# Moving four modulation units from the first MLP to the Hyena block of a diffusion backbone

## What is computed

```python
def adaln(cond, w, b):
    return jnp.split(jax.nn.silu(cond) @ w + b, 6, axis=-1)     # w: 2048 x 12288, per layer
...
sh1, sc1, g1, sh2, sc2, g2 = adaln(c[:, None, :], mod_w[l], mod_b[l])
...
# layer 1 (odd):
y = hyena_mixer(modulate(x, norm_mix_g[l], sh1, sc1), od_w_in[o], ...)
x = x + g1 * (y @ od_w_out[o])
x = x + g2 * ffn(modulate(x, norm_ffn_g[l], sh2, sc2), ffn_w1[l], ffn_w2[l])
...
def hyena_mixer(h, w_in, conv_w, conv_b, filt, skip):
    p = depthwise_conv(h @ w_in, conv_w) + conv_b
    x0, x1, v = jnp.split(p, 3, axis=-1)
    return x0 * bidir_long_conv(x1 * v, filt, skip)
def ffn(h, w1, w2):
    return jnp.square(jax.nn.relu(h @ w1)) @ w2
```

## Time and profile before

| | |
|---|---|
| median of 3 runs | 2666.0 us |
| profiled execution: device time | 2669.68 us |
| its span, first to last instruction | 2667.9 us |
| PE busy | 2517.2 us (94%) |
| DVE busy | 1812.4 us (68%) |
| ACT busy | 955.7 us (36%) |
| moved from memory | 611.40 MB, 229 GB/s |
| mean granted TensorE clock | 0.969 |
| first MLP, from its first to its last matmul | 694.11 to 1441.75 us |
| Hyena block, from its first matmul to the output projection's first | 1456.51 to 1797.61 us |

### The profile page before, as it was taken

One profiled execution on the slowest core, in us unless ns is written; L12 is line 12 of the kernel. 1 busy time (PEld: TensorE's weight loads), 2 busy tenths in 40 slices (PEclk: granted clock), 3 DMA queues, 4 the chain that ended last, 5 costly groups with the idle time before them and its releaser, 6 DMA issues.

```text
span 2667.9 us, 48783 instructions
## 1 busy us (share of the span) xinstructions
PE 2517.2 (94%) x19040; PEld 2327.9 (87%) x19040; DVE 1812.4 (68%) x2645; ACT 955.7 (36%) x958; POOL 0.2 (0%) x4
## 2 busy tenths in 40 slices
PE   6897978999899999999998999999899999999997
PEld 1223956999899999999998999899899999999997
DVE  1314765998788787787887787786677655555555
ACT  1313333333443343333434322233343343433333
POOL 0000000000000000000000000000000000000000
PEclk9788989999899999999998999999899999999998
DMA  8455724999688888888886555664588655555552
GB/s 278 144 170 188 251 97 159 340 335 334 220 291 295 292 294 299 281 297 291 288 298 215 208 195 189 228 231 154 189 274 273 202 175 186 185 177 189 177 185 94
DMA packets 266384, 611.40 MB, mean 229 GB/s; under 512 B 12245, under 2 KB 12373, under 8 KB 266014
## 3 DMA queue, kind: packets, MB, share of 16 engines
q1 hardware_dynamic: 260766, 598.93, 65.4%
q10 hardware_dynamic: 5504, 10.83, 1.2%
HBM read 603.43 MB, written 6.29 MB: 229 GB/s over the span
## 4 chain that ended last, share of the span: by engine, by line
PE 86%; DVE 7%; DMA 2%; issue 2%; ACT 2%; DVEq 0%; SPq 0%; ACTq 0%
PE acc L507 74%; PE acc L568 4%; PE aux L556 1%; DMA w_raw<-od_w_in 1%; DVE w_lo L766 1%; PE aux L712 1%; PE aux L504 1%; ACT w_hi L1213 1%; PE aux L732 1%; PE aux L545 1%; DMA scr<-k_freq 1%; DVE m_raw L774 1%; PE acc L674 1%; DVE x L849 0%; PE aux L548 0%
## 5 line engine op out<-in xcount | busy, mean ns | idle before, releaser
L766 DVE TENSOR_TENSOR w_lo<-w_raw,w_hi 128x2048 fp32r<-128x2048 f32 x372 | 851.1, 2289 | 491.0 <-ACT w_hi L1213 483.5
L1213 ACT ACTIVATE w_hi<-w_raw 128x2048 fp32r<-128x2048 f32 x372 | 712.0, 1915 | 1229.0 <-PE acc L507 1161.2
L507 PE MATMUL acc<-act_a,w_hi 128*128 128x256 f32 x6784 | 879.1, 286 | 29.6 <-DVE act_a L887 14.5
L507 PEld LDWEIGHTS acc<-act_a,w_hi 128*128 128x128 f32 x6784 | 850.0, 194 | 36.1 <-issue 19.7
L507 PE MATMUL acc<-act_b,w_hi 128*128 128x256 f32 x5120 | 643.1, 284 | 3.5 <-DVE summed L806 2.4
L507 PEld LDWEIGHTS acc<-act_b,w_hi 128*128 128x128 f32 x5120 | 627.2, 192 | 5.7 <-DVE x L849 2.6
L507 PE MATMUL acc<-act_a,w_lo 128*128 128x256 f32 x3392 | 448.7, 283 | 0.0
L507 PEld LDWEIGHTS acc<-act_a,w_lo 128*128 128x128 f32 x3392 | 426.6, 192 | 0.0
L507 PE MATMUL acc<-act_b,w_lo 128*128 128x256 f32 x2560 | 333.2, 283 | 0.0
L507 PEld LDWEIGHTS acc<-act_b,w_lo 128*128 128x128 f32 x2560 | 318.7, 192 | 0.0
L774 DVE SCALAR_TENSOR_TENSOR m_raw<-m_raw,wide 128x1024 f32<-128x1024 f32 x176 | 211.9, 1217 | 0.4
(11 more groups left out here) (131 smaller groups left out, 923.8 us busy)
## 6 DMA issues: line engine op xcount, KB each, us to landing
w_raw<-ffn_w SPq DMA_DIRECT2D x256, 1024.0 KB, 6.7
m_raw<-mod_rest SPq DMA_DIRECT2D x176, 512.0 KB, 5.6
scr<-mod_rest SPq DMA_DIRECT2D x144, 512.0 KB, 6.4
w_raw<-od_w_in SPq DMA_DIRECT2D x48, 1024.0 KB, 8.5
w_raw<-ev_w_in SPq DMA_DIRECT2D x36, 1024.0 KB, 9.2
w_raw<-mod_first SPq DMA_DIRECT2D x32, 1024.0 KB, 5.2
w_raw<-ev_w_out SPq DMA_DIRECT2D x16, 1024.0 KB, 9.3
w_raw<-od_w_out SPq DMA_DIRECT2D x16, 1024.0 KB, 5.2
```

Source lines behind the costliest of these rows:

```text
L507: mm = pe.matmul(acc[ft][:, 0:n], w, rhs[:, k, a:a + n], start=start, stop=stop)
L766: TT(w_lo[:, kg % 2, :], w_raw[:, kg, :], w_hi[:, kg % 2, :].bitcast(F32), ALU.subtract)\
L1213: return act.activation(out_, in_, func, **kw)
```

## The change

Per pass of the first MLP four modulation units are loaded and multiplied in place of five (32 tiles over eight units: four to a unit, in place of five), so 16 in place of 20. Per pass of the Hyena block it is two in place of one (16 tiles over three units: five, five and six, in place of two, three and three), so 8 in place of 4. The second MLP keeps its four. The total of tiles, of bytes and of matmuls stays the same. The Hyena block keeps its two slots.

```diff
--- before.py
+++ after.py
@@ -66,7 +66,7 @@
 
 
 MU_F0 = 12
-MU_D = 32
+MU_D = 28
 MU_F1 = 36
 
 
@@ -449,20 +449,20 @@
                     unit(u + n, w, row, col + n % 4 * 512, mods(mu, share(n, 8, count)),
                          mods(mu, share(n - 1, 8, count)) if n else before)
 
-            mlp_mods(0, U_F0, 0, 0, MU_F0, 5, ())
+            mlp_mods(0, U_F0, 0, 0, MU_F0, 4, ())
             with sp.Fori(1, 4) as q:
-                mlp_mods(q, q * 8 + U_F0, 0, 0, q * 5 + MU_F0, 5, mods(q * 5 + (MU_F0 - 5), share(7, 8, 5)))
+                mlp_mods(q, q * 8 + U_F0, 0, 0, q * 4 + MU_F0, 4, mods(q * 4 + (MU_F0 - 4), share(7, 8, 4)))
 
             def hyena(j, before, old=NARROW):
                 for n, col in enumerate((1, 2, 0)):
                     unit(j * 3 + (U_D - 3 + n), od_w_in, 0, j * 512 + (col * D_MODEL - 512),
-                         mods(j + (MU_D - 1), share(n, 3, 1)),
-                         mods(j + (MU_D - 1), share(n - 1, 3, 1)) if n else before, slots=NARROW, old=None if n else old)
-
-            hyena(1, mods(MU_D - 5, share(7, 8, 5)), WIDE)
+                         mods(j * 2 + (MU_D - 2), share(n, 3, 2)),
+                         mods(j * 2 + (MU_D - 2), share(n - 1, 3, 2)) if n else before, slots=NARROW, old=None if n else old)
+
+            hyena(1, mods(MU_D - 4, share(7, 8, 4)), WIDE)
             with sp.Fori(2, 5) as j:
-                hyena(j, mods(j + (MU_D - 2), share(2, 3, 1)))
-            unit(U_ODOUT, od_w_out, 0, 0, (), mods(MU_F1 - 1, share(2, 3, 1)), slots=NARROW)
+                hyena(j, mods(j * 2 + (MU_D - 4), share(2, 3, 2)))
+            unit(U_ODOUT, od_w_out, 0, 0, (), mods(MU_F1 - 2, share(2, 3, 2)), slots=NARROW)
             with sp.Fori(1, 4) as m:
                 unit(m + U_ODOUT, od_w_out, 0, m * 512)
             sp.wait_ge(b_made, 96)
@@ -1117,7 +1117,7 @@
             dve.wait_ge(mv_ready, 12)
             next_input(2, 32, 0, 48, "ffn_g")
             with own.loop(4, 0) as q:
-                mlp_mods(q, q * 8 + U_F0, 0, 16, q * 5 + MU_F0, 5, MU_F0, q * 4 + 4, q * 17 + 51)
+                mlp_mods(q, q * 8 + U_F0, 0, 16, q * 4 + MU_F0, 4, MU_F0, q * 4 + 4, q * 17 + 51)
             dve.wait_ge(mv_ready, MU_D)
             next_input(3, 48, 1, 96, "mix_g")
 
@@ -1178,7 +1178,7 @@
             def hyena(j, first=False):
                 for n, post in enumerate((x1_in, v_in, x0_in)):
                     body(j * 3 + (U_D + n), lambda: sums(j * 3 + (U_D + n)), lambda: post(j),
-                         j + MU_D, share(n, 3, 1), slots=NARROW,
+                         j * 2 + MU_D, share(n, 3, 2), slots=NARROW,
                          mid=None if n or first else (lambda: convolved(j - 1)))
                 product(j)
```

## The result

The changed kernel takes 2708.61 us (median of 4 runs, 2706.08 to 2711.29) where the kernel before takes 2665.38 (4 runs): 1.0164 times as long, 95% interval 1.0148 to 1.0181, or +43.2 us. The kernel before was measured beside every group of experiments, and its four medians lie between 2664.64 and 2666.16 us, so a difference between two kernels that weren't measured side by side is good to about 1.5 us. The forecast was 2690 us in a range of 2674 to 2711: slower, as forecast, and inside the range, but near its top, 18.6 us above the point.

A forecast was written before the change was run, and what follows sets the result against it. Both stages were taken to run close to their TensorE matmuls, so only gaps count. First MLP -10.7 us and Hyena block +34.4 us gave +23.7 us: 2690 us for the median, range 2674 to 2711 us.

The forecast's parts named there:

- The Hyena block: Sixteen tiles a pass for eight make SP hold the next weights behind tile waits; passes become 96.6 us, +34.4 us in all.
- inverse to v: Hyena pass, inverse transform to v's start on TensorE: 26.2 us in place of 18.5, v's weights held behind tile 1.
- v to x0: Hyena pass, v's start to x0's: 26.4 us, where it takes 25.2 now, by the same chain of held weights.
- x0 to the next inverse: Hyena pass, x0's start to the next inverse: 44.0 us, late weights hidden by the Fourier matmuls.
- first pass's inverse, later by: Hyena block's first pass, with no convolution ahead of its tile 1: its inverse comes 4.4 us late.
- the landing: Hyena weights, 1 MB, land 6.5 us after issue, with ends 5.2 and 7.8 giving the block +24 and +45 us.
- the forecast's upper end: Slowest landing of 1 MB of Hyena weights, 7.8 us, giving the block +45 us.
- the second rival: Hyena block: cold clock behind gaps adds some 8 us and slow landing of 7.8 us adds 10: 2708 us; chance 0.18.
- The first MLP: Four tiles a unit for five make the fetch ready 1.15 us sooner, so TensorE's gaps go: -10.7 us.
- Short landing: Hyena weights land as those that stand alone, 5.2 us, so +13.3 us in all: 2679 us; chance 0.17.
- Faster, with weights not held: Hyena block: SP passes tile waits before weights are wanted, only the first MLP's gain is left: 2655 us; chance 0.06.
- The rival with the MLP's gaps kept: First MLP's long gaps come from the loop's jump and stay, only 2.3 us saved there: 2698 us; chance 0.05.

The follow-up runs named there:

- e3: Kernel after, with SP issuing a Hyena unit's tiles 2 and 3 behind the next unit's first weights, 4 and 5 behind its second: 2671.38 us, 1.0027 times before.
- e4: Kernel after, with the x1 unit's second quarter of tiles (one tile) multiplied on DVE ahead of the convolution, not behind it: 2700.48 us.
- e5: Kernel after without the loads of the Hyena block's tiles; DVE still does all 64 multiplications, on other data: 2659.89 us, 0.9978 times before.
- e1: Kernel before with only the first MLP's half of the change, four units a pass; four modulation units left out: 2661.58 us, 0.9986 times before.
- e2: Kernel before with the first MLP's eight unrolled TensorE units a pass made two loops of one unit: 2657.34 us, 0.9976 times before.
- e9: Kernel before with the second MLP's two TensorE loops of one unit unrolled to eight units a pass: 2688.97 us, 1.0081 times before.
- e11: Kernel after with loops of one unit on TensorE in the first MLP, nothing else: 2696.76 us, 1.0113 times before.
- e10: Kernel before with TensorE's first MLP in loops of two units: 2656.77 us, 0.9969 times before.
- e8: Kernel after with one-unit TensorE loops in the first MLP, Hyena tiles issued later on SP, x1's second-quarter tile ahead of the convolution: 2655.59 us, 0.9958 times before.
- e7: Kernel after with one-unit TensorE loops in the first MLP and Hyena tiles issued behind the next weights on SP: 2661.63 us, 0.9985 times before.

## Why the prediction was right, and where it was short

**Direction and mechanism: right, shown.** SP's queue holds the weights behind tile waits, tile 1 stands behind the convolution, DVE's idle time takes the multiplications. e3 (order alone, -37 us), e4 (the gap ahead of v from 8 to 2.2 us) and e5 (multiplications alone cost nothing) each bear on one of these.

**The Hyena block: +34.4 forecast, +41.7 measured.** Step by step, in the three passes after the first inverse:

| step | forecast | measured |
|---|---|---|
| inverse to v | 26.2 | 27.5, 26.4, 26.1 |
| v to x0 | 26.4 | 28.1, 27.7, 26.8 |
| x0 to the next inverse | 44.0 | 44.0, 45.1, 44.1 |
| first pass's inverse, later by | 4.4 | 5.7 |

The chain of additions held; the mis-sized term is the landing, which I put at 6.5 us from the earlier trace rows. Two loads behind a tile in the kernel after, the first ahead of v, the second ahead of x0:

```profile
w_raw<-od_w_in SPq DMA_DIRECT2D x1, 1024.0 KB, 6.6
```

```profile
w_raw<-od_w_in SPq DMA_DIRECT2D x1, 1024.0 KB, 8.0
```

6.6 us is the first, in the pass whose v came 26.4 us after the inverse; where v came after 27.5 it was 7.5, and in the third pass 6.4. Ahead of x0 it was 8.0, 7.7 and 6.7; why those are the slower ones, no row here tells. The mean of the six is 7.2, and the forecast's upper end, 7.8, was the nearer one for two of the three ahead of x0. By the forecast's own 8 us for one us of landing, the 0.7 us make some 5 of the 7.3 us that were missing. The cold clock came as the second rival had it: 6.61 and 6.64 us for the first 32 matmuls behind two of the gaps, 5.3 to 5.6 behind the five others of 2.2 us or more. Of these the ones ahead of v were hidden; ahead of x0 the 6.64 goes with the one step of 45.1 us.

**The first MLP: -10.7 forecast, -0.2 measured.** This is the step that failed, and it is the larger miss. I read the late fetch beside the gap and took it for its cause; the row on which I rested that, the second MLP's first pass without a gap, has no late fetch, but it also has another loop on TensorE, and that I set aside as a rival at 0.05. e1 shows that the gaps stay when the fetch is in time, e2 and e9 that they go and come with the long loop's jump. The gaps were also taken too long: the 6.9 us at the boundaries and the 0.57 us in mid-pass are what lies between the chain's pieces, and TensorE's idle time is 5.5 us at the three boundaries and 0.1 us in mid-pass. What the late fetch does cost is the 3.6 us between e2 and e11. The size of the whole was right, by another split: short loops (-6.7 us) and four tiles (-3.6) together bring the stage from 762.4 to 752.1 us, -10.3, but the change had only the second of the two, and in the profiled execution of the kernel after most of that went into a second pass that starts at the lower clock behind its gap (184.64 us for 183.15) and into longer gaps.

**The other rivals.** Short landing (2679) is out by the landings of 6.4 to 8.0 us. Faster, with weights not held, is out by SP's 80.7 us. The time came out where the second rival had put it, 2708 us, but only in part for its reasons: about 7 us are landing and clock, about 10 the MLP's saving that didn't come. The rival with the MLP's gaps kept, at 0.05, is the one that came true, though the 2.3 us that it still allowed came to 0.2. That two misses with the same sign ended inside the range, 2.4 us below its top, is partly luck: no rival had the two together.

## What to carry to other kernels

A queue that issues both the loads that the bound engine lives on and side loads with few slots is an order to be read line by line: each side load with a wait ahead of it holds everything behind it, and moving it behind the next important load gave 37 of 43 us here, at the price of one tile that lands late. When a gap has a late engine beside it, ask what would end last if that engine were in time, and look for a place in the trace that differs in that one thing alone; a second place that differs in two proves neither. Here the middle of a pass was that place, with the late engine and without the jump. Read a gap as the engine's idle time, not as what lies between two pieces of the chain. And a gain on paper of removing work comes only where the wait that ends last is the one that the work feeds.

## What the runs showed of the hardware

- A loop on TensorE whose body is eight unrolled units (some 3000 matmuls and weight loads) costs 1.5 to 2.2 us of idle at a jump back in one stage (once 3.9), and 4.3 to 4.7 us in another, with 0.84 to 0.9 MB more on the instruction queue; bodies of one or two units cost nothing that shows (e2, e10).
- 1 MB from memory lands 5.2 us after its issue where loads come one by one, and 6.4 to 8.0 us with a tile ahead of it and two more weight loads 3.4 to 5.7 us behind, ahead of v and x0 in the kernel after. The Trainium skill, DMA: Bandwidth & Descriptors, Anatomy of one DMA, has 2.0 us and the bytes at 436 GB/s, by estimate 4.4 us, for a DMA that GpSimd issues. These are issued by SP, so the 4.4 us that the prediction took from that page are for another path; the quickest load of weights in the kernels before and after took 4.9 us.
- The first 32 matmuls behind a gap took 4.1 us after 1.95, 2.18 and 2.22 us of idle (e8, e4, e3) and even after 3.28 (e7), 5.3 to 5.7 after most gaps of 1.85 to 8 us, and 6.4 to 6.6 after 3.22, 3.83, 4.81 and 8.85: the length of the gap doesn't fix the price.
